# Gated linear attention with its state carried every 128 steps instead of 64, in a two-block transformer kernel

## The reference, cut to what matters

```python
b = jnp.cumsum(logf.reshape(B, H, N, CHUNK, DK), axis=3)
b_last = b[:, :, :, -1:, :]
b_mid = b[:, :, :, CHUNK // 2 - 1:CHUNK // 2, :]
A = einsum('bhntd,bhnsd->bhnts', q * exp(b - b_mid), k * exp(b_mid - b)) * mask
o_intra = einsum('bhnts,bhnsv->bhntv', A, v)
kv = einsum('bhnsd,bhnsv->bhndv', k * exp(b_last - b), v)
# state of chunk n+1 = exp(b_last of n) * state of chunk n + kv of n
o_inter = einsum('bhntd,bhndv->bhntv', q * exp(b), s_before)
out = o_intra + o_inter
```

## Time and profile before

| | |
|---|---|
| median of 3 executions | 1592.99 us (1592.9 to 1593.37) |
| the profiled execution | 1592.33 us, span of its records 1591.0 us |
| TensorE busy | 1577.2 us, 99% of the span |
| VectorE busy | 894.7 us, 56% |
| ScalarE busy | 661.8 us, 42% |
| mean granted TensorE clock | 0.997 of full speed |
| DMA | 144.25 MB, mean 91 GB/s |

### The profile page before, as it was taken

One profiled execution on the slowest core, in us unless ns is written; L12 is line 12 of the kernel. 1 busy time (PEld: TensorE's weight loads), 2 busy tenths in 40 slices (PEclk: granted clock), 3 DMA queues, 4 the chain that ended last, 5 costly groups with the idle time before them and its releaser, 6 DMA issues.

```text
span 1591.0 us, 17878 instructions
## 1 busy us (share of the span) xinstructions
PE 1577.2 (99%) x7432; PEld 1297.5 (82%) x7432; DVE 894.7 (56%) x1194; ACT 661.8 (42%) x808; POOL 14.0 (1%) x29
## 2 busy tenths in 40 slices
PE   8999999999999999999999999999999999999998
PEld 7787777888888888888898888888888888888887
DVE  7776677764444422368636643364436887776323
ACT  5757667432232221265433433234335444344212
POOL 2000000000000000000000000000000000000000
PEclk9999999999999999999999999999999999999999
DMA  6311101233333232232321233223322323223222
GB/s 198 91 63 53 54 27 61 73 105 106 93 106 104 82 106 92 94 126 72 120 80 54 66 100 106 80 80 106 102 71 93 106 82 104 93 93 119 82 104 80
DMA packets 119343, 144.25 MB, mean 91 GB/s; under 512 B 6097, under 2 KB 106288, under 8 KB 119264
## 3 DMA queue, kind: packets, MB, share of 16 engines
q1 hardware_dynamic: 118032, 139.96, 26.8%
q0 software_dynamic: 1232, 3.16, 0.6%
HBM read 141.01 MB, written 2.10 MB: 90 GB/s over the span
## 4 chain that ended last, share of the span: by engine, by line
PE 95%; DVE 2%; ACT 2%; issue 1%; DMA 0%; SPq 0%; DVEq 0%; ACTq 0%
PE bank L405 29%; PE bank L406 28%; PE bank L407 28%; PE bank L966 1%; PE bank L748 1%; PE bank L730 1%; PE bank L729 1%; PE bank L949 1%; PE bank L794 1%; PE bank L1029 0%; PE bank L789 0%; PE bank L757 0%; PE bank L739 0%; PE bank L776 0%; ACT h_hi L2523 0%
## 5 line engine op out<-in xcount | busy, mean ns | idle before, releaser
L1141 DVE TENSOR_TENSOR slab_lo<-slab_raw,slab_hi 128x2048 fp32r<-128x2048 f32 (+2 forms) x128 | 291.5, 2278 | 313.0 <-ACT slab_hi L2007 312.6
L405 PE MATMUL bank<-h_hi,slab_hi 128*128 128x512 f32 x1160 | 458.3, 395 | 0.2 <-DVE slab_lo L1141 0.2
L407 PE MATMUL bank<-h_hi,slab_lo 128*128 128x512 f32 x1160 | 452.1, 390 | 0.0
L406 PE MATMUL bank<-h_lo,slab_hi 128*128 128x512 f32 x1160 | 451.8, 389 | 0.0
L2007 ACT ACTIVATE slab_hi<-slab_raw 128x2048 fp32r<-128x2048 f32 (+1 forms) x127 | 240.8, 1897 | 172.8 <-DMA slab_raw<-in_w_down 142.3
L405 PEld LDWEIGHTS bank<-h_hi,slab_hi 128*128 128x128 f32 x1160 | 218.1, 188 | 46.8 <-issue 1.5
L407 PEld LDWEIGHTS bank<-h_hi,slab_lo 128*128 128x128 f32 x1160 | 218.0, 188 | 45.9
L406 PEld LDWEIGHTS bank<-h_lo,slab_hi 128*128 128x128 f32 x1160 | 218.2, 188 | 45.2 <-issue 1.2
L1187 DVE TENSOR_TENSOR tmp<-bank,x_rstd_rows 128x512 f32<-128x512 f32 x98 | 66.6, 687 | 100.9 <-PE bank L407 100.7
L405 PE MATMUL bank<-slab_hi,h_hi 128*128 128x256 f32 (+1 forms) x224 | 75.4, 337 | 0.0
L407 PE MATMUL bank<-slab_hi,h_lo 128*128 128x256 f32 (+1 forms) x224 | 73.6, 328 | 0.0
(11 more groups left out here) (442 smaller groups left out, 2218.8 us busy)
## 6 DMA issues: line engine op xcount, KB each, us to landing
slab_raw<-in_w_in SPq DMA_DIRECT2D x39, 1024.0 KB, 5.0
slab_raw<-in_w_up SPq DMA_DIRECT2D x33, 1024.0 KB, 5.0
slab_raw<-in_w_down SPq DMA_DIRECT2D x22, 1024.0 KB, 4.9
slab_raw<-in_w_gate SPq DMA_DIRECT2D x11, 1024.0 KB, 5.1
slab_raw<-in_w_o SPq DMA_DIRECT2D x4, 1024.0 KB, 4.9
slab_raw<-in_w_ple_gate SPq DMA_DIRECT2D x4, 1024.0 KB, 4.7
slab_raw<-in_w_ret_o SPq DMA_DIRECT2D x4, 1024.0 KB, 4.7
slab_raw<-in_w_sgu_o SPq DMA_DIRECT2D x4, 1024.0 KB, 4.7
```

The lines of the kernel that those rows point to most:

```text
L405: T.matmul(ps, a_hi, b_hi, start=start, stop=False, skip_group_check=skip)
L406: T.matmul(ps, a_hi, b_lo, start=False, stop=False, skip_group_check=skip)
L407: return T.matmul(ps, a_lo, b_hi, start=False, stop=stop, skip_group_check=skip)
L1141: V.tensor_tensor(w_lo[j][:, 0:n], raw[j][:, 0:n], w_hi[j][:, 0:n].bitcast(F32), ALU.subtract).then_inc(slab_lo, 1)
```

## The change

`gla_decay`, the reset table and the scan go from 64-step chunks to 128-step chunks (one per tile of 128 steps): three chunk sums with 128 rows instead of seven with 64, a copy and two multiply-adds for the states instead of a copy and six, three products for the outputs of the states instead of seven. The scores within a 128-step tile still come from the two 64-step squares (scaled around their own middles); the block between the two (later queries, earlier keys) is a product of its own: VectorE makes a third difference into tmp[6] (`cross_all`, sums less the sum at the border), ScalarE two exponentials of 128x256 from it (exponential 4 and 5 of the now seven of a direction), VectorE multiplies them with queries and keys in `decayed_keys`, TensorE makes two 128x128 products in bank 5 within `intra`, between the scores and the transposes, and ScalarE copies two pieces of 64 rows by 128 columns from them into the score tile (`crossed`, after `keys`, before `split`). The next user of bank 5 and `outputs` wait for those copies.

```diff
...
     reset = np.ones((P, S))
-    reset[:, ::HG_CHUNK] = 0.0
+    reset[:, ::P] = 0.0
     mix1 = np.concatenate([perm, maskf, maskb, reset], 1)
...
     ones_r = sb("ones_rounded", [P, P], F32R)
-    decs = sb("gla_decay", [P, 2, NCH])
+    decs = sb("gla_decay", [P, 2, TT])
     ln_stats, ln_mv, ln_rs = sb("ln_stats", [P, 8, 6]), sb("ln_mean_var", [P, 8, 2]), sb("ln_rstd", [P, 8])
...
     kd_t = per_tile(slot("gla_keys_t", 42, 1)[:, 0, :])
-    st = sb("gla_states", [P, NCH, P], at=tmp_end - 2 * BLK)
+    st, cross_all = sb("gla_states", [P, TT, P], at=tmp_end - BLK), tmp[6]
+    cross = [cross_all[:, half * CW:(half + 1) * CW] for half in range(2)]
+    early = [slice(HG_CHUNK * back, HG_CHUNK * (back + 1)) for back in range(2)]
+    late = early[::-1]
...
     gla_scan, gla_exps, gla_decayed = sem("gla_differences"), sem("gla_exps"), sem("gla_decayed")
-    gla_states, gla_keys = sem("gla_states"), sem("gla_keys")
+    gla_states, gla_keys, gla_crossed = sem("gla_states"), sem("gla_keys"), sem("gla_crossed")
     gla_squared, gla_summed, gla_rstd = sem("gla_squared"), sem("gla_squares_summed"), sem("gla_rstd")
...
         def intra(n):
-            k = zt[:, 4 + 4 * (n % 2) + n // 2, :]
+            k, back = zt[:, 4 + 4 * (n % 2) + n // 2, :], n % 2
             ps = take(("gla_a", n), 6)
...
             whole(("gla_a", n), ins)
+            ps = take(("gla_x", n), 5, gla_crossed, 2 * n + 2)
+            for two in range(2):
+                ins = T.matmul(ps[:, chunk[two]], cross[back][:, chunk[two]], cross[1 - back][:, chunk[two]], start=two == 0,
+                               stop=True, skip_group_check=True)
+            whole(("gla_x", n), ins)
             ps = take(("gla_kt", n), 2)
...
                 T.wait_ge(tile["hi", hd // 2, t].free, tile["hi", hd // 2, t].value)
-            bs = [take(("gla_kv", n, half), 2 + half, gla_states, n + 1) for half in range(2)]
-            own = range(1, NCH) if back else range(NCH - 1)
-
-            for c in own:
-                half = c % 2
-                rws = slice(HG_CHUNK * half, HG_CHUNK * (half + 1))
-                ins = T.matmul(bs[half][:, chunk[c // 2]], kd_t[rws, c // 2, :], v_hg[rws, c // 2, hd * P:(hd + 1) * P],
-                               start=c < own[0] + 2, stop=True, skip_group_check=True)
-            whole(("gla_kv", n, 1), ins)
+            ps = take(("gla_kv", n), 3, gla_states, n + 1)
+            own = range(1, TT) if back else range(TT - 1)
+
+            for j in own:
+                ins = T.matmul(ps[:, chunk[j]], kd_t[:, j, :], v_hg[:, j, hd * P:(hd + 1) * P], start=j == own[0], stop=True,
+                               skip_group_check=True)
+            whole(("gla_kv", n), ins)
...
             T.wait_ge(tile["gla_a", n].free, tile["gla_a", n].value)
+            T.wait_ge(gla_crossed, 2 * n + 2)
             T.wait_ge(gla_states, n + 1)
...
                          start=not back and j == 0, stop=False, skip_group_check=True)
-            for c in range(NCH):
-                if c != (NCH - 1 if back else 0):
-                    rws = slice(HG_CHUNK * (c % 2), HG_CHUNK * (c % 2 + 1))
-                    ins = T.matmul(ps[rws, chunk[c // 2]], qb[:, c * HG_CHUNK:(c + 1) * HG_CHUNK], st[:, c, :], start=False,
-                                   stop=True, skip_group_check=True)
+            for j in range(TT - 1) if back else range(1, TT):
+                ins = T.matmul(ps[:, chunk[j]], qb[:, chunk[j]], st[:, j, :], start=False, stop=True, skip_group_check=True)
             passed(("gla_out", n), ins)
...
             back, bb = n % 2, decay[n]
-            mid, end = (HG_CHUNK // 2, 0) if back else (HG_CHUNK // 2 - 1, HG_CHUNK - 1)
-            at = lambda c: chunks(bb)[:, :, c:c + 1].broadcast_to([P, NCH, HG_CHUNK])
+            mid, last, end = (HG_CHUNK // 2, HG_CHUNK, 0) if back else (HG_CHUNK // 2 - 1, HG_CHUNK - 1, P - 1)
             V.wait_ge(log_done, n + 1)
...
                 V.wait_ge(psum_ready, tile["gla_kt", n - 1].done)
-            V.tensor_tensor(chunks(ki), chunks(bb), at(mid), ALU.subtract).then_inc(gla_scan, 1)
-            V.tensor_tensor(chunks(kd), at(end), chunks(bb), ALU.subtract).then_inc(gla_scan, 1)
+            V.tensor_tensor(chunks(ki), chunks(bb), chunks(bb)[:, :, mid:mid + 1].broadcast_to([P, NCH, HG_CHUNK]),
+                            ALU.subtract).then_inc(gla_scan, 1)
+            V.tensor_tensor(per_tile(kd), per_tile(bb)[:, :, end:end + 1].broadcast_to([P, TT, P]), per_tile(bb),
+                            ALU.subtract).then_inc(gla_scan, 1)
+            halves = bb.rearrange("p (j h t) -> p h j t", h=2, t=HG_CHUNK)
+            V.tensor_tensor(cross_all.rearrange("p (h j t) -> p h j t", h=2, t=HG_CHUNK), halves,
+                            per_tile(bb)[:, :, last:last + 1].unsqueeze(1).broadcast_to([P, 2, TT, HG_CHUNK]),
+                            ALU.subtract).then_inc(gla_scan, 1)
...
             V.wait_ge(z_act, q_ready[n // 2])
-            V.wait_ge(gla_exps, 5 * n + 1)
+            V.wait_ge(gla_exps, 7 * n + 1)
             decayed_step[n] = step(V.tensor_tensor(qi, qi, zt[:, n // 2, :], ALU.mult))
...
             V.wait_ge(key_done, n + 1)
-            V.wait_ge(gla_exps, 5 * n + 3)
+            V.wait_ge(gla_exps, 7 * n + 5)
+            back, q = n % 2, per_tile(zt[:, n // 2, :])
+            e, l = per_tile(cross[back]), per_tile(cross[1 - back])
+            V.tensor_tensor(l, l, q[:, :, late[back]], ALU.mult)
+            V.tensor_tensor(e, e, per_tile(k)[:, :, early[back]], ALU.mult)
             V.wait_ge(vector_step, step(V.tensor_tensor(kd, kd, k, ALU.mult)))
...
         def decayed(n):
-            V.wait_ge(gla_exps, 5 * n + 5)
+            V.wait_ge(gla_exps, 7 * n + 7)
             V.tensor_tensor(decay[n], decay[n], zt[:, n // 2, :], ALU.mult).then_inc(gla_decayed, 1)
...
         def state_updates(n):
-            V.wait_ge(psum_ready, tile["gla_kv", n, 1].done)
-            V.wait_ge(gla_exps, 5 * n + 4)
-            for i in range(NCH - 1):
-                c = NCH - 1 - i if n % 2 else i
-                to = c - 1 if n % 2 else c + 1
-                kv = tile["gla_kv", n, c % 2].ps[:, chunk[c // 2]]
+            V.wait_ge(psum_ready, tile["gla_kv", n].done)
+            V.wait_ge(gla_exps, 7 * n + 6)
+            for i in range(TT - 1):
+                j = TT - 1 - i if n % 2 else i
+                to = j - 1 if n % 2 else j + 1
+                kv = tile["gla_kv", n].ps[:, chunk[j]]
                 if i == 0:
...
                 else:
-                    ins = V.scalar_tensor_tensor(st[:, to, :], st[:, c, :], decs[:, n % 2, c:c + 1], kv, ALU.mult, ALU.add)
-                if i < NCH - 2:
+                    ins = V.scalar_tensor_tensor(st[:, to, :], st[:, j, :], decs[:, n % 2, j:j + 1], kv, ALU.mult, ALU.add)
+                if i < TT - 2:
                     V.wait_ge(vector_step, step(ins))
...
         def decays(n):
-            A.wait_ge(gla_scan, 2 * n + 1)
+            back = n % 2
+            A.wait_ge(gla_scan, 3 * n + 1)
             A.activation(qi, ki, ACT.Exp).then_inc(gla_exps, 1)
-            A.wait_ge(gla_exps, 5 * n + 1)
+            A.wait_ge(gla_exps, 7 * n + 1)
             A.activation(ki, ki, ACT.Exp, scale=-1.0).then_inc(gla_exps, 1)
-            A.wait_ge(gla_scan, 2 * n + 2)
+            A.wait_ge(gla_scan, 3 * n + 2)
             A.activation(kd, kd, ACT.Exp).then_inc(gla_exps, 1)
+            A.wait_ge(gla_scan, 3 * n + 3)
+            A.activation(cross[1 - back], cross[1 - back], ACT.Exp).then_inc(gla_exps, 1)
+            A.activation(cross[back], cross[back], ACT.Exp, scale=-1.0).then_inc(gla_exps, 1)
+
+        def crossed(n):
+            back, x = n % 2, tile["gla_x", n]
+            A.wait_ge(psum_ready, x.done)
+            A.wait_ge(tile["gla_a", n].free, tile["gla_a", n].value)
+            for b in range(2):
+                src = x.ps[b * HG_CHUNK:(b + 1) * HG_CHUNK, 0:2 * P].rearrange("p (two c t) -> p two c t", two=2, c=2)[:, :, b, :]
+                dst = a_t.rearrange("p (two c t) -> p two c t", two=2, c=2)[early[back], :, b, late[back]]
+                A.activation(dst, src, ACT.Copy).then_inc(gla_crossed, 1)
         def chunk_decays(n):
-            bb, end = decay[n], 0 if n % 2 else HG_CHUNK - 1
+            bb, end = decay[n], 0 if n % 2 else P - 1
             if n >= 2:
                 A.wait_ge(gla_states, n - 1)
-            A.activation(decs[:, n % 2, :], bb.rearrange("p (c t) -> p c t", t=HG_CHUNK)[:, :, end:end + 1]
+            A.activation(decs[:, n % 2, :], bb.rearrange("p (c t) -> p c t", t=P)[:, :, end:end + 1]
                          .rearrange("p c t -> p (c t)"), ACT.Exp).then_inc(gla_exps, 1)
-            A.wait_ge(gla_exps, 5 * n + 4)
+            A.wait_ge(gla_exps, 7 * n + 6)
             A.activation(bb, bb, ACT.Exp).then_inc(gla_exps, 1)
...
             if n:
-                A.wait_ge(psum_ready, tile["gla_kv", n - 1, 1].done)
```

(2 more changed lines are left out.)

## The result

| | before | after |
|---|---|---|
| median (lowest to highest, executions) | 1593.23 us (1592.9 to 1593.82, 6) | 1599.99 us (1599.3 to 1600.93, 6) |
| the profiled execution, its span | 1592.33, 1591.0 us | 1599.85, 1598.5 us |
| TensorE busy | 1577.2 us | 1575.3 us |
| VectorE, ScalarE busy | 894.7, 661.8 us | 893.9, 672.0 us |
| mean granted clock | 0.997 | 0.995 |

The ratio of the times is 1.0042, 95% interval 1.0032 to 1.0053. The forecast was 1599.5 us. The sum came out, but only because errors of opposite sign in its terms cancelled each other; most of what follows is about that.

What follows compares the result with a forecast made beforehand. TensorE, busy in 99% of the span, was taken to bound the kernel; 8.3 us of added waits less 1.2 us of its work gave +7.1 us, so 1599.5 us, own range 1597.5 to 1601.5.

Steps and rivals of the forecast that it cites:

- TensorE's work: Per direction, eight full products replace fourteen half-array ones at 0.15 us each: -0.15 us, -1.2 us in all.
- (a): Before round 0: two added ScalarE exponentials lie in the softmax chain TensorE already waits for, +0.64 us.
- (b): Last softmax unit of rounds 0, 1, 2: two added VectorE products delay the softmax weights, 3 x 0.66 = +1.98 us.
- (c): Round 5: ScalarE's added copies and exponentials delay the transposed weights that a value product awaits, +1.0 us.
- (d): Rounds 6 and 7: TensorE waits for round 7's keys, +1.5 us, then the new product for bank 5, +3.2 us.
- rival 1: TensorE's clock falls to half speed around the two waits of round 7: 1602.5 us, chance 0.28.
- rival 2: Bank 5 is free in time in round 7, so no second wait: 1596.3 us, chance 0.15.
- Rival 3: Half-array products do not really pair, so the change saves 11.8 us of TensorE's work: 1588.8 us, chance 0.04.
- Rival 4: VectorE's and ScalarE's additions are hidden and only the -1.2 us stays: 1591.1 us, chance 0.08.

Runs made afterwards that it cites:

- the keys edit: Changed kernel with VectorE copying head 2's output before preparing round 7 and reducing it before the split, ScalarE's two Silus after round 7's chunk decays: 1594.08 us.

## Why the prediction was right, and where it was wrong

| step | predicted | measured |
|---|---|---|
| TensorE's work | -1.2 (-2.6 to +0.8) | -5.3 |
| (a) before round 0 | +0.64 | +0.62 |
| (b) rounds 0, 1, 2 | 3 x 0.66 | 0.68, 0.64, 0.68 |
| (c) round 5 | +1.0 | +1.5 |
| (d) keys 7 | +1.5 | +2.2 |
| (d) bank 5 | +3.2 | +3.2 |
| clock | 0 (rival 1: +3.0) | +1.7 |
| start of the execution | 0 | +1.3 in this one |
| sum | +7.1 | +5.9, with the start +7.2 |

The waits are measured from start to start. The spans give 7.5, of which 0.2 lie behind the stage.

**The failed step** is TensorE's work: "So a half product costs 0.15 us and a full one 0.245", and from it -0.15 per direction. Both prices are off. A full product of this size steps 0.22 (0.111 an instruction), which stood in the rows as the lower bound, and a pair of halves the same. The slots that I divided hold the fixed price of a group of halves, and the part of it on the neighbours I had taken for the neighbours' own cost: the chunk sums fell from 1.09 to 0.59, the outputs from 1.02 to 0.67, the scores product before them from 0.98 to 0.89, the linear attention scores after them from 1.00 to 0.89 (where they follow directly; transposes from 0.49 to 0.44), the entry into the chunk sums from 0.95 to 0.86; the new group cost 0.45, not 0.49. That is -0.63 or -0.69 a direction, -5.3 in all. The groups' own slots make -3.2 of it, already past my lower bound, because three sums take 0.59 where I had at least three steps of 0.22; the other -2.1 lie in the neighbours' slots, which both bounds left as they were. The earlier trace rows even had the hint: the same scores product takes 1.00 after halves, and in the earlier trace rows 0.89 after transposes.

**(a) and (b)** came out in mechanism and size: the exponentials step 0.31 each, the 256-wide products of VectorE 0.34 and 0.33, and each chain has them in full.

**(c)** has the right chain, sized too small. ScalarE's stretch from `keys` to `transposed` grew from 8.60 to 10.07 us: 0.73 for the copies (0.5 predicted) and 0.72 for the exponentials with the step out of them (0.64). The two 64x128 copies take 0.59 together, and `keys` ahead of them steps 0.62 where it had 0.48. By an estimate from the Trainium skill ("ScalarE: Activation LUTs", What ACT_TABLE_LOAD costs: 186 ns + 0.833 ns an element, less 93 ns of overlap) a copy is 0.20, and the trace, with 0.29, differs from it by more than from my 0.25; for a 128x256 exponential the same estimate is 0.31, and the trace agrees. And TensorE, which I had 0.13 later, was done with its work ahead of L751 as long after the start of `keys` as before (8.93 us for 8.95).

**(d), first wait.** From `masked(6)` on (263.27 before, 264.88 after) keys 7 are 1.91 us later (277.02 and 280.54, less 1.61); predicted were 1.9. But TensorE was ready for them 0.67 us earlier on the same way (14.30 us after `masked(6)` for 14.97), predicted 0.15, and it started 0.14 us after the keys were done, predicted 0: 0.7 us more of wait. The wait is where its gain goes. **Second wait:** the bank is free at 285.42, TensorE's start moved by 3.22, as predicted; the holder and the place were right, and rival 2 (the bank free in time) fell.

**Rival 1** (the clock) happened, in addition to the waits of the forecast and not at its price: 6.8 us at 1.2 GHz, as in the earlier trace rows, but TensorE idled through 2.8 us of it, and the 0.6 us before that were spent in the scores product, ahead of a wait that took up the loss; 1.7 us lost where I had 3.0. I gave it 0.28 and kept it out of the sum; it belonged in it. My argument against it, that 0.9 us of products between the waits would hold the clock, is refuted: it fell in the middle of those products. **Rival 3** (halves do not pair) is wrong as a mechanism, since they pair exactly, though it pointed to the right side: TensorE's gain was more than four times mine. **Rival 4** (hidden) fell with every wait of (a) to (d).

The errors: 4.1 us too little gain against 1.2 too little wait ((c), (d)), 1.7 of clock and, in the profiled execution, 1.3 at its start. That 1599.5 met 1599.99 is luck, owed to their meeting. The sign was less so: with the 8.3 us of waits that I had and the measured -5.3 it is still slower, by 3.0. But it hangs on (d): the runs that take either wait of (d) away, at 1.0011 and 1.0009, lie within 0.2% of the kernel before.

What stays open: whether the higher executions of the kernels with one wait are those in which the clock fell (one such was profiled, for the keys edit), and what decides it.

## What to carry to other kernels

Price a small product by its instruction's step and look at the slots of its neighbours; a slot divided by its count hides a fixed cost of the group, and the neighbours pay part of it. If TensorE's own work shrinks ahead of waits whose ends are set by VectorE's and ScalarE's programs, the gain is swallowed: first put their programs in an order in which the late operand comes first, then count the gain (here 5.3 us less of work became 6.8 us of loss, and with the orders changed 6.3 us of gain, of which the orders give 1.5 without the change). For each product that a change adds, look up which tile holds its PSUM bank at that moment and where in the other engine's program it is read.

## What the hardware showed that I had not expected

- A group of f32 products on half of the array costs 0.1 us on the product before, 0.16 inside and 0.1 on the product after (0.05 where transposes follow), the same for six halves and for twelve; within it pairs run at the price of a full product (0.217 against 0.22).
- A single wait of 2.0 us can cost the clock or not: in one profiled kernel it held 1.00 through it, in another 3.4 us at 1.2 GHz followed. Two waits of 2.0 and 2.8 us gave 6.8 us of it, 2.0 and 2.1 in another kernel more still (0.74, 0.50, 0.73 over 15 us, or 10.3 us at 1.2 GHz).
- The start of an execution scatters by more than a microsecond: in the thirteen profiled executions TensorE's products reach their step of 0.23 us at 9.65 to 13.56 us. The two kernels with chunks of 64 steps began the stage earliest of all; two executions do not show whether that is more than scatter, as each of them was 0.8 to 0.9 us under its kernel's median.
